# Two-block transformer on one core: products pass by pass, and a new order of the first mixer's output product, its border and the attention's copies and splits

## The reference

```python
def first_block(x, p, ...):
    h = x
    z = rms_norm(h, g_mix_pre) @ w_in
    conf_ab, q, k, v, f_logit, sc_h, sc_b, sc_c, pool_v = jnp.split(z, ...)
    y_conf = conformer_conv(conf_ab, ...)        # a*sigmoid(b), 31-tap conv, layer norm, silu, @ w_pw
    y_att = forgetting_attention(q, k, v, ...)   # 4 heads of 64, softmax with decay
    y_sc = short_conv_mixer(sc_h, sc_b, sc_c, w_sc)   # bg * conv3(cg * h)
    y_pool = multiscale_pool(pool_v, w_pool, pool_scale)
    mix = concatenate([y_conf, y_att, y_sc, y_pool]) @ w_out     # 4 x 256 rows of w_out
    h = h + rms_norm(mix, g_mix_post)
    h = h + rms_norm(square(relu(rms_norm(h, g_mlp_pre) @ w_up)) @ w_down, g_mlp_post)
    gate = sigmoid(rms_norm(h, g_ple_pre) @ w_ple_gate)
    return h + rms_norm((p @ w_ple_proj) * gate, g_ple_post)

def second_block(x, ...):
    for l in range(2):
        hn = rms_norm_2(x, norm_mix[l])
        m = attention_mixer(hn, ...) if l % 2 == 0 else recurrent_mixer(hn, ...)
        x = x + m
        x = x + swiglu(rms_norm_2(x, norm_ffn[l]), ...)
    return rms_norm_2(x, norm_final)
```

## Time and profile before

| | us |
|---|---|
| median of three runs | 1016.58 (1016.34 to 1019.48) |
| the profiled execution | 1014.87 |
| its span, first to last instruction | 1013.1 |
| PE / DVE / ACT busy | 957.2 / 702.1 / 507.8 |

### The profile page before, as it was taken

The page is one execution under the profiler, slowest core; times in us unless marked ns, Lnnn a source line. Parts: engine busy times, 40 slices in busy tenths (PEclk is TensorE's granted clock), DMA queues, the critical chain, the costliest instruction groups (busy, mean ns, idle before and its releaser), DMA issues.

```text
span 1013.1 us, 13530 instructions
## 1 busy us (share of the span) xinstructions
PE 957.2 (94%) x5540; PEld 837.1 (83%) x5540; DVE 702.1 (69%) x942; ACT 507.8 (50%) x677; POOL 68.6 (7%) x89
## 2 busy tenths in 40 slices
PE   6987899999999989979999999999989899999997
PEld 5986798888888779858988888888989789888886
DVE  4599566666667876975676666666979676666663
ACT  4755554444445637665544434357644354444341
POOL 4120010000001100100000000010122100000000
PEclk9998999999999989999999999999999999999999
DMA  9734336656654435321566556565521356555531
GB/s 321 235 127 124 117 123 212 204 166 202 209 170 175 140 107 174 131 76 61 181 218 207 196 179 208 167 189 166 166 85 42 125 166 208 180 195 192 182 125 42
DMA packets 106190, 164.40 MB, mean 162 GB/s; under 512 B 2816, under 2 KB 82784, under 8 KB 106000
## 3 DMA queue, kind: packets, MB, share of 16 engines
q1 hardware_dynamic: 104688, 158.25, 47.7%
q0 software_dynamic: 1440, 5.28, 1.5%
HBM read 162.47 MB, written 1.05 MB: 161 GB/s over the span
## 4 chain that ended last, share of the span: by engine, by line
PE 70%; DVE 18%; ACT 5%; issue 4%; DMA 2%; POOL 1%; DVEq 0%; SPq 0%; POOLq 0%; ACTq 0%
PE ps L380 68%; DVE wl L1699 6%; DVE SC L1799 2%; PE ps L388 2%; ACT wh L1141 1%; DMA raw<-in_w_in 1%; DVE xhl L1704 1%; DVE xf L1708 1%; ACT junk L1129 1%; DVE st L2102 1%; POOL st L2458 1%; DVE rows L2301 1%; DVE h L1761 0%; DMA prm<-in_prm 0%; ACT SC L1452 0%
## 5 line engine op out<-in xcount | busy, mean ns | idle before, releaser
L1699 DVE TENSOR_TENSOR wl<-raw,wh 128x2048 fp32r<-128x2048 f32 (+2 forms) x150 | 339.1, 2263 | 162.5 <-ACT wh L1141 162.2
L1141 ACT ACTIVATE wh<-raw 128x2048 fp32r<-128x2048 f32 (+2 forms) x150 | 282.0, 1885 | 167.9 <-PE ps L380 148.0
L380 PE MATMUL ps<-xhl,wh 128*128 128x512 f32 (+1 forms) x1248 | 281.4, 353 | 5.9 <-DVE wl L1699 3.5
L380 PE MATMUL ps<-wh,xhl 128*128 128x512 f32 (+3 forms) x1000 | 252.5, 343 | 13.3 <-issue 5.7
L380 PEld LDWEIGHTS ps<-xhl,wh 128*128 128x128 f32 x1248 | 216.5, 193 | 33.6 <-DVE wl L1699 4.1
L380 PEld LDWEIGHTS ps<-wh,xhl 128*128 128x128 f32 x1000 | 172.6, 192 | 33.9 <-issue 5.9
L380 PE MATMUL ps<-xhl,wl 128*128 128x256 f32 x1008 | 173.1, 283 | 0.0
L380 PE MATMUL ps<-wl,xhl 128*128 128x512 f32 (+3 forms) x500 | 169.9, 340 | 0.0
L380 PEld LDWEIGHTS ps<-xhl,wl 128*128 128x128 f32 x1008 | 150.4, 191 | 7.5
L380 PE MATMUL ps<-wh,fh 128*128 128x512 f32 x304 | 118.9, 391 | 1.8 <-DVE fl L1949 1.5
L380 PE MATMUL ps<-wh,fl 128*128 128x512 f32 x304 | 118.7, 390 | 0.0
(11 more groups left out here) (266 smaller groups left out, 821.3 us busy)
## 6 DMA issues: line engine op xcount, KB each, us to landing
raw<-in_ffn_gate SPq DMA_DIRECT2D x22, 1024.0 KB, 5.2
raw<-in_ffn_up SPq DMA_DIRECT2D x22, 1024.0 KB, 5.2
raw<-in_ffn_down SPq DMA_DIRECT2D x22, 1024.0 KB, 4.9
raw<-in_w_up SPq DMA_DIRECT2D x16, 1024.0 KB, 5.5
raw<-in_w_down SPq DMA_DIRECT2D x16, 1024.0 KB, 4.8
raw<-in_s_w_in SPq DMA_DIRECT2D x14, 1024.0 KB, 5.3
raw<-in_w_in SPq DMA_DIRECT2D x9, 1024.0 KB, 7.1
raw<-in_a_w_in SPq DMA_DIRECT2D x6, 1024.0 KB, 5.2
```

What stands on the lines that cost most here:

```text
L380: return e.matmul(o, a, b, start=start, stop=stop, skip_group_check=True)
L1141: e.activation(high_of(i), raw_of(i), ACT.Copy).then_inc(*up("act_high", i))
L1699: e.tensor_tensor(low_of(i), raw_of(i), high_of(i).bitcast(F32), ALU.subtract).then_inc(*up("dve_lo", i))
```

## The change

1. `feat`, `feat_parts`, `tok`, `project`, `project_half` and `project_end` go through a slot pass by pass: all xh·wH, all xl·wH, all xh·wL. They wait for `act_high` ahead of the first pass and for `dve_lo` only ahead of the last. Where a caller gives `x_low`, the wait for the low half of the activation stands ahead of the second pass, and the caller itself waits for the high half only. The number of products and weight loads is the same, 5540 each.
2. In the first mixer all three lists are in another order: ACT's `pool_out` and part 3's high half come before the exps and the short tap, the weight halves 11 and 12 later; DVE's low half of part 3 comes before the short taps, `short_out` before `forget_max(2)`, the low half of slot 11 behind the last tap; PE goes on in the order shown below.
3. At the border to the first FFN slot 14's high half goes behind `norm_squares`, its low half behind `norm_rows`.
4. In the attention ACT's tick 7 goes behind both groups of turned copies, `highs` of the output product's second weight goes from tick 11 to tick 9, its lows from ahead of tick 7 to tick 8 and from tick 9 into `map_mean(7)`.
5. The gate, the FFN heads, `wide` and the output products of attention and recurrent mixer give `x_low` as in 1.

```diff
 def tok(i, outs, tb, k0=0, first=True, final=True, x=(xh, xl), x_low=None):
+    if tb == 0:
+        e.wait_ge(*at("act_high", i))
+    for o, c in outs:
+        for k in range(kt):
+            mm(o, x[0][:, k0 + k, s], wH[:, k, c], first and k == 0, False)
+    if x_low:
+        e.wait_ge(*x_low)
+    for o, c in outs:
+        for k in range(kt):
+            mm(o, x[1][:, k0 + k, s], wH[:, k, c], False, False)
     if tb == 0:
         e.wait_ge(*halves_ready(i))
     for o, c in outs:
         for k in range(kt):
-            d = mm3(o, x[0][:, k0 + k, s], x[1][:, k0 + k, s], wH[:, k, c], wL[:, k, c], ...)
+            d = mm(o, x[0][:, k0 + k, s], wL[:, k, c], False, final and k == kt - 1)
...
 # PE, first mixer's output product
-e.wait_ge(*at("dve_mix_low", 3, 0))
-project(1, sl, 3, 0, order)
+e.wait_ge(*at("dve_short_in"))
+e.wait_ge(*at("act_part_high", 1, 3, 0))
+project(1, sl, 3, 0, order, at("dve_mix_low", 3, 0))
 ...
 forget_mix(0)
-conformer_mean()
 project(1, sl, 2, 0, ...)
 forget_turn(2); forget_mix(1)
+project(1, sl, 3, 1, order); conformer_mean(); project(1, sl, 2, 1, order)
 conformer_variance(); forget_turn(3); forget_mix(2); forget_mix(3)
-project(1, sl, 3, 1, order)
 project(1, sl, 1, 0, ...)
 conformer_out()
-project(1, sl, 2, 1, order); project_half(1, sl, 0, 0, 0 and 1); project(1, sl, 1, 1, order)
-norm_turn(1, 0); project_half(1, sl, 0, 1, 0 and 1)
+project(1, sl, 1, 1, order); project_half(1, sl, 0, 0, 0 and 1); project_half(1, sl, 0, 1, 0)
+norm_turn(1, 0); project_half(1, sl, 0, 1, 1)
...
 # PE, wide (attention's first products); the gate and the FFN heads likewise
-e.wait_ge(*at("dve_xl", n, 0, 1))
+e.wait_ge(*at("act_xh", n, 0, 1))
...
 # ACT and DVE, border to the first FFN
-highs(14)
 post_squares(1, 0); norm_squares(1, 0)
-highs(UP["ff"][0][0])
+highs(UP["ff"][1][0])
 norm_high(1, 0)
-lows(14)
 post_rows(1, 0); norm_rows(1, 0)
-lows(UP["ff"][0][0])
+lows(UP["ff"][1][0])
 norm_low(1, 0)
...
 # DVE, attention
+                        if i == 7:
+                            lows(S["aout"][0])
...
                 tick(6, do)
-                lows(S["aout"][3])
                 for t in range(7, 16):
                     tick(t, do)
-                    if t == 9:
-                        lows(S["aout"][0])
+                    if t == 8:
+                        lows(S["aout"][3])
```

More of the change, by code:

```diff
@@ L465, in project_end @@
                     if (tb, half) == (0, 0):
+                        e.wait_ge(*at("act_high", sl[i]))
+                    for x in (xh, xl):
+                        for k in range(2):
+                            mm(o, x[:, 2 * i + k, s], wH[:, k, c], False, False)
+                    if (tb, half) == (0, 0):
                         e.wait_ge(*halves_ready(sl[i]))
                     for k in range(2):
-                        d = mm3(ps[ACC[n][tb][half]][:, :], xh[:, 2 * i + k, s], xl[:, 2 * i + k, s], wH[:, k, c], wL[:, k, c],
-                                False, i == order[3] and k == 1)
+                        d = mm(o, xh[:, 2 * i + k, s], wL[:, k, c], False, i == order[3] and k == 1)
                     if (tb, half) == (1, 1):
@@ L755, in gate @@
                     project_half(3, S["gate"], 3, 0, half)
-                e.wait_ge(*at("dve_xl", 2, 1, 1))
+                e.wait_ge(*at("act_xh", 2, 1, 1))
                 for i in order[:3]:
-                    project(3, S["gate"], i, 1, order)
+                    project(3, S["gate"], i, 1, order, at("dve_xl", 2, 1, 1) if i == order[0] else None)
                 project_half(3, S["gate"], 3, 1, 0)
@@ L1270, in forget_probs @@
                     d.then_inc(*up("act_forget_probs", i))
+                e.wait_ge(*at("pe_pool"))
+                for t in range(2):
+                    e.activation(xf[:, 6 + t, :], ps[2][:, 256 * t:256 * t + 256], ACT.Identity, scale=P("pool_scale", t)).then_inc(
+                        *up("act_pool_out", t))
                 forget_exp(0)
@@ L1275, in first_mixer @@
                 forget_probs(1)
+                e.wait_ge(*at("pe_slot", S["sb"]))
+                e.wait_ge(*at("act_pool_out", 1))
+                for tb in range(2):
+                    part_high(6, 8, tb, (1, 3, tb))
                 e.wait_ge(*at("dve_short_in"))
@@ L1886, in first_mixer @@
                 taps(1, 18, 20)
+                mix_low(3)
                 for t in range(2):
@@ L1900, in first_mixer @@
                     *up("dve_short_out"))
+                forget_max(2)
+                taps(1, 20, 22)
+                forget_inverse(2)
                 forget_max(3)
-                taps(1, 24, TAPS)
+                mix_low(2)
+                taps(1, 22, 26)
                 forget_inverse(3)
-                mix_low(2)
+                taps(1, 26, TAPS)
+                lows(11)
                 e.wait_ge(*at("pe_conf_mean"))
```

137 lines of the change are left out of this document (69 added, 68 removed).

## The result

The changed kernel took 1009.26 us (median of four runs, 1007.75 to 1010.59), the kernel before 1017.33 in the same comparison (1016.34 to 1019.48). The ratio is 0.9918, with a 95% interval of 0.9905 to 0.9932: 8 us faster, and 1008.8 had been forecast. The two numbers, 8 and 5.7, are not the same, and in the first mixer the way there is not the one that the forecast took.

The account below looks back on a forecast made before the run. PE, busy 94% of the span, bounds the long FFNs, so gains come only where PE stands idle or slow: 2.6 + 2.5 + 2.7 = 7.8 us off the median 1016.58 gives 1008.8; range 1004.0 to 1013.0.

Parts of the forecast that it names:

- Part 1, the border to the attention: At 359.90: product starts without waiting for split wl, 1.7 us, plus 0.8 from the clock; 2.5 us (1.7 to 3.3).
- Part 2, the first mixer: Output product starts at 87.3, 5.2 us sooner; 2.6 us remain at the gain behind the border (1.4 to 4.0).
- the second of the three: First mixer: part 3/1 moves ahead of the mean into idle time, so conformer_out moves from 113.96 to about 110.1, 3.8 us.
- The split at the border: Border to first FFN: slot 14's split (2.29) between hs and gain, less 0.36 idle, delays the gain 1.9 to 2.0 us.
- The clock at 127.76: Pause before the border's turns grows from 3.75 to 4.4 us; if the clock falls, 0 to 1.4 us are lost.
- Part 4, the attention: Earlier turned copies bring map 8's logits 2.6 us sooner, DVE's split is covered at 433 to 436; 2.7 us (1.0 to 4.0).
- B: Rival: half given back, DVE bounds the first mixer and the attention trades one tick's wait for the next; 1012.9, chance 0.20.
- A: The forecast itself, all three gains as worked out: 1008.8 us, own range 1005.8 to 1011.5, chance 0.57.
- E: Rival: slower, clock stays at 1.2 GHz through the first mixer's short pieces between 87 and 118; 1020, chance 0.04.
- C: Rival: first pass starts early but PE stops before the third, so nothing ends sooner; about 1015, chance 0.11.
- D: Rival: more gained, mixer keeps 4.0 us, clock stays up at 433; about 1004.5, chance 0.08.
- signs of being wrong: Second block's turns at 140 or later, a 0.5 clock between 98 and 120, or map 8's idle time back before map 9 or 10.

Follow-up runs that it names:

- e2: Kernel before with only the pass-by-pass products and later waits, all lists in the old order; ratio 0.9972 to the kernel before.
- e6: Changed kernel with the new orders of the first mixer and of its border to the first FFN undone; ratio 0.9951 to the kernel before.
- e1: The changed kernel run again, nothing altered, as reference point; ratio 0.9922 to the kernel before.
- e4: Changed kernel with the attention's copies, weight halves and splits back in the old order; ratio 0.9952 to the kernel before.
- e5: The kernel before profiled once more, nothing altered; the execution took 1016.34 us with a span of 1014.5.
- e11: Changed kernel keeping, in the attention, only tick 7 behind both groups of turned copies, weight halves and splits in the old order; ratio 0.9921 to the kernel before.
- e7: Changed kernel with PE's conformer_mean ahead of part 3/1 and conformer_variance ahead of part 2/1; ratio 0.9942 to the kernel before.
- e12: Changed kernel with slot 14's split in its old place and 6, 8 and 4 idle products in three PE pauses; ratio 0.9886 to the kernel before, median 1005.73 us.
- e3: Changed kernel with slot 14's high and low halves back ahead of post_squares and post_rows at the border; ratio 0.9925 to the kernel before.
- e8: Changed kernel with conformer mean and variance sooner in PE's list and slot 14's split in its old place; ratio 0.9931 to the kernel before.

## Why the prediction was right, and where it was not

The time and the sign were right. In the timed runs so were the sizes of the three parts: 2.5, 2.6 and 2.7 us forecast, 2.8 (e2), 2.9 (e6 against e1) and 3.0 (e4 against e1) measured, each known to 1 to 2 us. The path in the first mixer was wrong in one step.

- **Part 1, the border to the attention: 2.5 forecast, 3.3 measured.** The mechanism is right. The product starts 0.85 us behind the turns and not 2.72, so 1.9 us (1.7 taken), and the clock stayed at 2.4 GHz behind them, which was taken at 0.8 and brought 1.4. In e1 and e4 the clock did fall there (8 products in 3.43 us at 356.83 in e1), and the stage still took only 63.2: part of the slow stretch lies where PE would wait for the second token block anyway, 0.67 us in the rows above. So the passes alone are worth 2.8 us there where the clock falls all the same, and 3.3 where it stays.
- **Part 2, the first mixer: 2.6 forecast; 0.6 in the pair of traces, 1.8 over repeated ones** (141.3 in before and e5, 139.5 in changed, e1, e4 and e11), **2.9 in the timed runs, there with part 3.** The start (87.3 forecast, 87.55) was right. The step that failed is the second of the three, 3.8 us at `conformer_out`: that with part 3/1 ahead of the mean there is less for PE to do, in time that was idle. It came 1.75 us sooner in the pair, and 2.5 over the same repeated traces (114.1 to 111.6). In the earlier trace rows DVE was idle, and I took PE's list for the cause. PE itself was not idle: between the first product of the output product and `conformer_out` it waited 0.75 and 0.86 us in 21.42 before (92.54 to 113.96), and 0.86, 0.93 and 0.92 in 24.66 now (87.55 to 112.21). The new order does not only move part 3/1 within this stretch, it also moves part 2/1 into it, which stood behind `conformer_out` before, and these 12 products take 2.96 us (102.47 to 105.43). The forecast never counted them, though the order shown under the change has them, and at its own price of 0.22 us they come to 2.6. So PE begins 5.0 us sooner and needs 3.2 longer, which leaves the 1.75. Part 1/1 went the same way, ahead of 0/0, so that behind `conformer_out` nothing is made good. e7 confirms that PE is full there; no run moved part 2/1 back, so that this would win anything is not shown.
- **The split at the border** cost what was worked out, 1.9 us from `post_rows` to the gain: 7.53 us in the changed kernel, 5.63 in the earlier trace rows and 5.64 in e12, both with turns of 1.09 us; 1.5 with slow turns (6.00 in e3). It is a loss in this stage that the change made itself, though the timed runs of e3 do not show it.
- **The clock at 127.76.** I read in the earlier trace rows that a pause of 3.75 us left the clock alone, and counted the trace against the page's rule. The forecast kept a fall for its lower end. The second execution, e5, has the same pause and slow turns behind it. One trace does not show what a pause does, only what it did. The rule of the Trainium skill ("TensorE: Matmul & The Clock Gate", section "Why this matters for your kernels") is that long pauses between bursts take the clock down. e5 and the changed kernel agree with it at this border (slow turns behind 3.75 and 4.34 us), and so does e12, where filling the pauses kept the clock at 1.00; the first trace does not.
- **Part 4, the attention: 2.7 forecast, 2.2 in the averages of the stage and 3.0 in the timed runs.** The size was right, the account too simple. The copies bring 1.8 and not 2.6 us, since tick 7's exp becomes last (0.6 had been counted for it, and off the path). And the cover named for DVE's split was the wrong one: the idle time of the earlier trace rows at 433 had shrunk to 1.64 us and ended at 429.92, and the split runs behind it, at 430.46. PE's wait at the next map is 2.37 us, where e11, without the moved splits, has 1.07. Behind that DVE does the second moved split, at 441.84, in `map_mean(7)`, where it waited 2.98 us in the earlier trace rows. In sum the moved copy and splits are not told from nothing (e11).
- **Part 1, the recurrent mixer: 0 forecast.** Right; 1.53 us of wait stand now where 0.79 stood. PE comes sooner and waits there instead.
- **The step from the profiled execution to the median** was right: 7.8 us taken off the median shown, and the timed runs have 8.0 to 8.5. The traces differ by 5.7 us because 1014.87 was a quick execution, which could not be known from one trace. That 1008.8 met 1009.26 to 0.5 us is in part luck: in the first mixer a gain at `conformer_out` that was forecast too large stands beside a clock that scatters by as much, and the runs tell the parts apart to no better than 1 us.
- Of the rivals, B came near in the first mixer, where PE waits somewhat more than before (2.7 us against 1.6 up to `conformer_out`), but B named DVE as what bounds it, and it is PE; the other parts went as in A. E, the slower clock spread over the mixer, happened for 8 products of one part. C and D did not happen. One of the signs of being wrong did come, the second block's turns at 140 or later (140.12); in e1, e4 and e11 they came at 139.2 to 139.5. The clock was 1.00 from 98 to 120, and of the wait before map 8 a part came back, the 2.37 us at 434.92.

What stays open: why a pause takes the clock down in one execution and not in the next. Whether e7 is slower than the changed kernel in fact (0.9942 against 0.9922) was not settled; the wait of 0.82 us in e8 speaks for it, but e7's own trace does not have it. The attention's own slow stretches (0.74 in the changed kernel between 430 and 437) were not filled, so what they cost was not measured.

```profile
430.00:437.00 7.00, 4.63 (x24) 3.89 (x23) 6.58 (x20) 5.12 (x10) 0.70 (x1) 0.74 0.44 144
```
